# Order of the three split terms in the feed-forward products: low weights second instead of third

## What is computed

```python
def swiglu(x, wi, wo):
    g, u = jnp.split(x @ wi, 2, axis=-1)
    return (jax.nn.silu(g) * u) @ wo

def ffn_half(h, m, k, g_norm, wi, wo):
    hn = modulate(rmsnorm_2(h, g_norm), m[3 * k], m[3 * k + 1])
    return h + 0.5 * m[3 * k + 2][:, None, :] * swiglu(hn, wi, wo)
```

## Time and profile before

| what | value |
|---|---|
| median of three runs | 3228.16 us |
| lowest and highest run | 3222.38 and 3233.09 us |
| profiled execution, span from first to last instruction | 3232.7 us |
| time of the profiled execution around its span | not recorded apart from the span |
| TensorE matmul busy | 2980.5 us (92%), 23333 matmuls |
| TensorE weight load busy | 2355.4 us (73%), 23333 loads |
| VectorE busy | 1466.3 us (45%) |
| ScalarE busy | 978.6 us (30%) |
| GpSimd busy | 366.3 us (11%) |
| mean granted TensorE clock | 0.959 of full speed |

### The profile page before, as it was taken

How to read it: one execution, slowest core, us unless ns; L and a number is a source line. 1 busy time by engine, 2 the same in 40 slices (tenths; PEclk the granted TensorE clock), 3 DMA queues, 4 the chain that set the end, 5 groups by cost and what they waited for, 6 DMA issues and landing times.

```text
span 3232.7 us, 54559 instructions
## 1 busy us (share of the span) xinstructions
PE 2980.5 (92%) x23333; PEld 2355.4 (73%) x23333; DVE 1466.3 (45%) x2114; ACT 978.6 (30%) x1442; POOL 366.3 (11%) x221
## 2 busy tenths in 40 slices
PE   6988777999999899899899989999899997999999
PEld 6876565677667599776566648888688886669899
DVE  6534243233233366582722234444544456571466
ACT  3211213222222244533621122222422224252343
POOL 5123000000000000131022100000000012215000
PEclk9999888999999999899999999999999998999999
DMA  6346858998989835321012212222222221204352
GB/s 240 137 165 254 338 218 348 415 370 341 391 344 375 361 144 182 118 78 53 1 53 102 81 65 92 95 100 92 75 95 91 98 97 65 91 15 182 143 185 90
DMA packets 77063, 547.73 MB, mean 169 GB/s; under 512 B 8385, under 2 KB 10433, under 8 KB 11057
## 3 DMA queue, kind: packets, MB, share of 16 engines
q1 hardware_dynamic: 76000, 540.05, 43.3%
q0 software_dynamic: 848, 4.52, 0.4%
HBM read 637.86 MB, written 1.05 MB: 198 GB/s over the span
## 4 chain that ended last, share of the span: by engine, by line
PE 81%; DVE 10%; ACT 4%; DMA 3%; issue 1%; POOL 0%; DVEq 0%; SPq 0%; POOLq 0%; ACTq 0%
PE bank L693 61%; PE bank L1037 8%; DMA ring<-slabs 3%; PE bank L1359 2%; DVE clow L2363 1%; ACT whi L1774 1%; ACT ht L1578 1%; PE bank L742 1%; DVE tiny L2516 1%; PE bank L872 1%; PE bank L1447 1%; PE bank L1428 1%; PE bank L859 1%; DVE wk L2493 1%; PE bank L709 1%
## 5 line engine op out<-in xcount | busy, mean ns | idle before, releaser
L693 PE MATMUL bank<-hhi,whi 128*128 128x256 f32 (+1 forms) x1408 | 482.5, 343 | 30.1 <-DVE hlo L1997 30.1
L693 PE MATMUL bank<-hlo,whi 128*128 128x256 f32 (+1 forms) x1408 | 476.9, 339 | 0.0
L693 PE MATMUL bank<-hhi,wlo 128*128 128x256 f32 (+1 forms) x1408 | 473.3, 336 | 0.0
L1977 DVE TENSOR_TENSOR wlo<-ring,whi 128x2048 fp32r<-128x2048 f32 x132 | 298.7, 2288 | 223.3 <-ACT whi L1547 196.2
L693 PE MATMUL bank<-fhl,whi 128*128 128x256 f32 (+1 forms) x1408 | 351.6, 341 | 0.0
L693 PEld LDWEIGHTS bank<-hhi,whi 128*128 128x128 f32 x1408 | 267.1, 190 | 70.2 <-issue 29.6
L1547 ACT ACTIVATE whi<-ring 128x2048 fp32r<-128x2048 f32 x132 | 251.2, 1908 | 218.3 <-PE bank L693 211.6
L693 PEld LDWEIGHTS bank<-hhi,wlo 128*128 128x128 f32 x1408 | 268.3, 191 | 30.2
L693 PEld LDWEIGHTS bank<-hlo,whi 128*128 128x128 f32 x1408 | 268.6, 191 | 26.3
L1037 PE MATMUL bank<-ring,wk 128*32 128x256 f32 x4064 | 256.2, 396 | 21.4 <-DMA ring<-slabs 13.1
L693 PEld LDWEIGHTS bank<-fhl,whi 128*128 128x128 f32 x1408 | 240.8, 188 | 35.4 <-issue 5.3
(11 more groups left out here) (440 smaller groups left out, 5147.3 us busy)
## 6 DMA issues: line engine op xcount, KB each, us to landing
ring<-slabs SPq DMA_DIRECT2D x542, 1024.0 KB
wk<-slabs SPq DMA_DIRECT2D x45, 1024.0 KB, 11.4
ac<-slabs SPq DMA_DIRECT2D x16, 1024.0 KB, 10.6
wk<-mixp POOLq DMA_DIRECT2D x1, 1040.0 KB, 12.6
xt<-xT SPq DMA_DIRECT2D x1, 1024.0 KB, 6.5
xt<-ctxT POOLq DMA_DIRECT2D x1, 1024.0 KB, 6.0
out<-xt SPq DMA_DIRECT2D x4, 256.0 KB, 2.4
cst<-maskc POOLq DMA_DIRECT2D x1, 960.0 KB, 14.4
```

The lines of the kernel that those rows point to most:

```text
L693: last = pe.matmul(o, a, b, start=k == 0, stop=k == len(pairs) - 1)
L1977: tt_(wlo_of(n), slab(n), whi_of(rel).bitcast(F32), ALU.subtract).then_inc(sem("wlo"), 1)
```

## The change

In both lists of pairs of `ffn(ph)` the second and third term of each channel tile change places. The same matmuls are issued, as many, with the same operands into the same banks. Within a channel tile, the old order keeps the stationary tile for two matmuls (high weights), then changes it; the new order keeps the moving operand for two matmuls (high activations), and has the stationary tiles high, low, high.

```diff
                         for k in range(KT):
                             hi, lo = halves(rel, k, ft * P, KT)
-                            pairs3 += [(hi, HHI[:, k, 0:T]), (hi, HLO[:, k, 0:T]), (lo, HHI[:, k, 0:T])]
+                            pairs3 += [(hi, HHI[:, k, 0:T]), (lo, HHI[:, k, 0:T]), (hi, HLO[:, k, 0:T])]
...
                             for k in range(FT):
                                 hi, lo = halves(rel, k, j * P, FT)
                                 fh, fl = FHI[b % 3][:, k, 0:T], FLO[b % 3][:, k, 0:T]
-                                pairs3 += [(hi, fh), (hi, fl), (lo, fh)]
+                                pairs3 += [(hi, fh), (lo, fh), (hi, fl)]
```

## The result

The changed kernel takes 3241.1 us (median of 20 runs) against 3227.28 us for the kernel before (20 runs). The ratio is 1.0045, with a 95% interval of 1.0035 to 1.0055: by this ratio 14.5 us slower, 11.3 to 17.7 (the two medians lie 13.8 us apart). The range of 3220 to 3245 us holds it, the likeliest case (3224 to 3238 us, within 0.3%) does not; it came out on the slower side, which had 0.18.

A forecast was written before the change was run, and what follows sets the result against it. TensorE's matmuls were taken to bound the kernel. Terms summed to 0 by kept transitions or +5.5 us by L1359's pace; the middle, +2.7, on 3228.2 gave 3230.9, say 3231 us, range 3220 to 3245 us.

The forecast's parts named there:

- the likeliest case: Whole kernel: no change within 0.3%, about 3231 us with an own range of 3224 to 3238 us; chance 0.73.
- What bounds the kernel: TensorE, busy 92% of the span; the four feed-forward phases lie whole in the chain, so matmul pace counts in full.
- Waits and queues at 0 us: Feed-forward phases: waits and signals stay at the same places, no DMA is moved, so 0 us.
- The first products at 512 tokens: 2112 matmuls of 512 columns, now 0.2289 us apart: 0 or +6.2 us, bounds -2.9 and +10.4 us.
- The first reading: First products, 512 tokens: the new order has the same three transitions of the moving operand, so 0 us; chance 0.36.
- The second reading: First products, 512 tokens: pace of the value product at L1359, 0.2318 us each, +6.2 us; chance 0.30.
- The first products at 256: 2112 matmuls of 256 columns: place in the triple makes no difference, 0 us, bounds -1.5 and +5.9 us.
- The down product: 1056 matmuls of each width: -0.7 us at 512 tokens (bounds -5.3, +1.4), 0 at 256 (-1.7, +1.3).
- The repeated stationary tile: Rival, both products: a weight tile used twice running is cheap and the change gives that up; 2.1 us, 3230 us, chance 0.03.
- The slower rival: First products lose their even pace and fall to 0.2338 and 0.120 us: 19.0 us in all, 3247 us; chance 0.18.
- The rule on separate read ports: TensorE: loading the next weights takes no read bandwidth from the running matmul, so pairing can't matter and the sum is 0.
- a cause that it hadn't counted: A granted clock below 1.00 in the blocks, or a change in stages the list doesn't touch; no size given.

## Why the prediction was right or wrong

*What bounds the kernel: right.* The phases are in the chain whole, and a change of pace of 3.6 ns in 2112 matmuls came through in full: 7.6 us in the earlier trace rows against the chain after.

*Waits and queues at 0 us: right.* The wait for HLO ahead of the 512-wide first products is 19.9 us against 19.7 in the earlier trace rows, the work of VectorE and ScalarE in a block is the same, and the counts are the same:

```profile
L693 PE MATMUL bank<-hhi,whi 128*128 128x512 f32 x704 | 282.0, 401 | 19.9 <-DVE hlo L1997 19.9
```

*The first products at 512 tokens: this step failed.* It offered two readings, 0 us by kept transitions of the moving operand and +6.2 us by the pace of L1359, and I took the middle. The first reading is refuted: it took the short distance for a property of HHI following HHI. In the new order HHI follows HHI as well, and there the distance is the longest, 0.2333 us. A distance depends on what streams and on what is loaded beside it, and on how their starts lie to each other; a list of regions on one side of the pair leaves out half of it. The second reading, from the nearest measured row, was nearly the size: 0.2318 against 0.2325 us, +6.2 against +7.6 us. The mean over both halved that term. But that L1359 came so near is in part luck: the order that it shares with the change doesn't set the pace by itself, since the same order runs at 0.2267 us with equal starts, and the down product had 0.2325 us in either order. The prediction had the thing in hand when it said that the two products differ in where their operands lie, and put no price on it.

*The first products at 256: mis-sized.* Taken at 0, since the place in the triple made no difference; measured 0.1171 to 0.1178 us, +1.6 us. An even average over the places says that no one distance is special. It doesn't say that another order keeps the sum.

*The down product: right.* 0.2326 us after 0.2325, where -0.7 us was taken; alone it measured no change.

*The repeated stationary tile: rightly set aside,* and now shown: the order without any repeated tile has the old pace. Its price was written wrongly: 352 x 2 + 704 x 2 is 2112, while the 2.1 us belong to 352 + 704 = 1056 matmuls of 512 columns. *The slower rival* (even pace lost) named the mechanism and the place, and priced it by the slowest neighbour, 0.2338 and 0.120 us, at 19 us; the blocks give 9.4. By blocks alone the change would have stayed just inside 0.3%, at 3237.6 us, and within 3224 to 3238 us; the measured 0.45% has 5 us more, most of which goes with the clock. So the wide range held the result because it allowed for half of the slower rival, not because the favoured readings were right, and part of the time came from stages that the change doesn't touch, which the prediction had named as a cause that it hadn't counted.

*The rule on separate read ports.* The Trainium skill (TensorE: Matmul & The Clock Gate, Step-by-step: what each phase is for) says that loading the next weights takes no bandwidth from the running matmul. With equal starts this case agrees in that the pairing doesn't matter: 0.2267 us in both orders tried. With unequal starts it doesn't: which tile is loaded beside which stream, and at which offset, moved the pace between 0.2267 and 0.2333 us at 512 columns. The measurement decides here.

## What to carry to other kernels

When only the order of matmuls changes and TensorE is the bound, read the distance from start to start for every pair of neighbours, in each shape, and take the pace of a stream that has the new kind of order and whose operands start alike, rather than a mean with an argument that nothing would change. Look at where the operands start within a partition before looking at their order: a pad of 96 bytes was worth 2.5% of the first products' time after the change at 512 columns, more than any order. And try a placement by shape, since what was best at 512 columns was the worst at 256. When a difference is a few tenths of a per cent, compare runs with the same mean granted clock: here 0.001 of it was worth some 2 us, as much as a fifth of the change.

## What the hardware showed that was not expected

- With stream and load starting equal modulo 512 bytes, matmuls on 128x128 tiles start 0.2267 us apart at 512 columns and 0.1200 us at 256, in both orders tried and at two offsets (128 and 160). With unequal starts it is 0.2289 to 0.2333 us at 512 and 0.1171 to 0.1191 us at 256 in the placements tried: slower at the one width, faster at the other.
- The six orders of three terms fall into two cycles. With HHI and the high weights at 32 and HLO and the low weights at 128 modulo 512, one sense of the cycle has 0.2289 us and the other 0.2325 us. The down product, with both activation parts at 32, has 0.2325 us in either.
- Runs of one kernel differ by some 20 us with the mean granted clock, some 2 us for 0.001 of it (0.958 to 0.966 in 38 runs of the kernel before), in stages where TensorE works in pieces.
